# The last hidden tile's squares, mixes and split one down unit later, and two parts of the fourth tile loaded ahead of others

## The chip, the core and the metric

The kernel runs on one core of one Trainium2 chip. Its time is the time of the device for one execution, in microseconds, and the figure compared is the median of several executions. TensorE (PE in the profile, its weight loads PEld) multiplies, VectorE (DVE) and ScalarE (ACT) do elementwise work, GpSimd (POOL) and SyncE (SP) issue the transfers (DMAs) here. Each engine runs its own list of instructions strictly in order, and waits where a semaphore is not yet as far as an instruction asks.

## What is computed

One decoder layer for a prompt of 512 tokens and 32 sample tokens, 544 together: four token mixers (pooling, a gated recurrence, two kinds of attention), then an MLP. Only the MLP matters here:

```python
h = rms_norm(x, norm2_g)                              # 544 x 2048
hid = relu(einsum('btd,df->btf', h, w_up))            # 544 x 8192
x = x + einsum('btf,fd->btd', hid * hid, w_down)      # 544 x 2048
```

Everything is float32. Each operand of a product is split into a high and a low part in a type that TensorE takes (fp32r), and a product is three matmul passes: high by high, high by low, low by high.

## The kernel before

**Seven products.** Both matrix products of the MLP go by a scheme that makes four output blocks from seven products instead of eight, named P1 to P7. A unit is one pair of output row blocks: units 0 to 31 (UP_UNITS = 32) make the 8192 hidden rows, two blocks of 128 rows by two halves of 272 tokens each; units 32 to 79 are the down projection. A down unit is 48 accumulation windows of eight pairs of output rows: unit 32 + s works for the row pair s mod 8 on the hidden tiles of `window(s)`. A hidden tile is what one up unit leaves: its seven operands, high and low (128 x 7 x 2 x 272 numbers, 1904 KB). Windows grow slowly at first: unit 32 takes tiles 0 and 1, unit 33 tiles 0 to 2, units 34 and 35 tiles 0 to 3, unit 36 tiles 0 to 4, unit 37 tiles 2 to 6. The number of tiles in a window is the unit's depth, and a product of depth d is three groups of d matmuls of 128 x 272. An up unit has depth 8.

**The order of products** is the list RUN. Within a unit v it is P1, P2, P6, P5, P7, P4, and P3 of unit v comes behind P1 of unit v + 1, except at unit 31, whose P3 comes ahead of P1 of unit 32. So around the turn TensorE runs: P4(31), P3(31), P1(32), P2(32), P6(32), P5(32), P7(32), P4(32), P1(33), P3(32), P2(33), P6(33), P5(33), P7(33), P4(33), P1(34), P3(33), P2(34). ACT and DVE walk through the same list in loops of their own (from L1583 and L2221), and what they do at a position is done when that product is finished.

**What hangs on a product.** Its weight operand's high part is made by ACT (`op_high_part`) and its low part by DVE (`op_low_part`), both four products ahead, in a ring of four, so that they wait for the product four places before. At P1, P6 and P7 ACT copies the accumulated bank into `lines` (`copy_line`, waited for by P6, P7 and the ends). DVE makes the sums of weight blocks for the next unit (`sum_1` at P6, `sum_2` at P5, `sum_3` at P7, `sum_4` at P1) and the outputs (`first_ends` at P7, `second_ends` at P3). P3 of a unit waits for its `first_ends`.

**The hidden tile of an up unit v.** ACT takes its relu at P4(v) (`first_relu`) and its squares at P3(v): `first_squares` waits until the store of tile v - 1 has landed (`hid_stored`), since `hid_out` is one buffer, and then `second_squares`; four ACT instructions. DVE makes four differences at P2(v + 1) (`mix_hidden`), ACT the high part at P6(v + 1) (`hidden_high`), DVE the low part at P5(v + 1) (`hidden_low`), and POOL stores the tile to DRAM (`store_hidden`).

**POOL's queue at the turn** (L1172 to L1193). Each product's region of `hid_in` lies where the up products' operands lay, so a region is loaded when the last up unit's product of that name is done (`load_first(o)`, tiles 0 and 1 for product o). `load_part(i, r)` loads tile i for region r: region 0 is P1 and P2 together and region 1 is P6 and P5 (544 KB each), regions 2, 3, 4 are P7, P4, P3 (272 KB each). Unit 32's product o waits for its own `load_first`. P1 of a later unit waits for all five parts of each tile that its window adds (`hid_loaded`, L2633). POOL issues in order, and a wait holds what stands behind it.

Of the kernel before, what the change touches and what calls it, by code (L numbers as in the profile page):

```python
# [55 lines left out]
UP_UNITS, DOWN_UNITS, ROW_PAIRS = 32, 48, 8  # L56
# [14 lines left out]
def window(s):  # L71
    return OPENS[s], OPENS[s + ROW_PAIRS]
# [3 lines left out]
FIRST_TILES = window(0)[1]  # L76


def user_of(i):
    return max(s for s in range(DOWN_UNITS) if window(s)[0] <= i)  # L80
# [3 lines left out]
P1, P2, P6, P5, P7, P4, P3 = range(7)  # L84
# [62 lines left out]
def build_step(nc, xT, w_forget, weights, w_early, params, consts, dconsts, pool_w, lru_w, state_pool,  # L147
# [877 lines left out]
    def _(pool):  # L1025
# [20 lines left out]
        for g in range(GT):  # L1046
            w = 2 ** (g + 1)
            u = proj[:, U_POOL, g]
# [84 lines left out]
        def store_hidden(u):  # L1133
            pool.wait_ge(*hid_ready.at(u + 1))
            pool.dma_start(hid_parts[u], hid_out[:].bitcast(F32)).then_inc(hid_stored, 16)
# [3 lines left out]
        def load_first(o):  # L1139
            r, a = IN_AT[o]  # L1140
            pool.wait_ge(*product_done.at(AT[LAST, o] + 1))
            pool.dma_start(hid_in[r][:, a, 0:FIRST_TILES].bitcast(F32),
                           hid_parts[0:FIRST_TILES, :, o].rearrange("q p i n -> p q i n")).then_inc(first_in[o], 16)
# [3 lines left out]
        def load_part(i, r):  # L1147
            last = REGIONS[r][-1]
            if i < HID_SLOTS:
                pool.wait_ge(*product_done.at(AT[LAST, last] + 1))  # L1150
            else:
                pool.wait_ge(*product_done.at(AT[UP_UNITS + user_of(i - HID_SLOTS), last] + 1))
            q = i % UP_UNITS
            pool.wait_ge(hid_stored, 16 * (q + 1))
            o, n = REGIONS[r][0], len(REGIONS[r])
            pool.dma_start(hid_in[r][:, :, i % HID_SLOTS].bitcast(F32), hid_parts[q, :, o:o + n]  # L1156
                           ).then_inc(hid_loaded[i % HID_SLOTS].s, 16)

        def load_hidden(i, first=0):
            for r in range(first, len(REGIONS)):  # L1160
                load_part(i, r)
# [12 lines left out]
        load_first(P1)  # L1174
        load_first(P2)
        load_part(FIRST_TILES, 0)
        load_first(P6)
        load_first(P5)
        load_part(FIRST_TILES, 1)
        store_hidden(LAST - 1)  # L1180
        for o in (P7, P4, P3):
            load_first(o)
        load_hidden(FIRST_TILES, 2)
        load_hidden(FIRST_TILES + 1)
        store_hidden(LAST)
        added_rows = 0
        for i in range(FIRST_TILES + 2, HID_LOADS):
# [9 lines left out]
    def _(act):  # L1197
        own = Own(act, act_own)

        def f(out, in_, func, **kw):  # L1200
            return nc.scalar.activation(out, in_, func, **kw)  # L1201
# [277 lines left out]
        for i in range(UNITS - 1):  # L1479
            u, odd = divmod(i, 2)  # L1480
# [82 lines left out]
        def first_squares(v):  # L1563

            act.wait_ge(*a_relu.at(v + 1))
            if v:
                act.wait_ge(hid_stored, 16 * v)
            f(hid_f[:, 0:7:6], ends_a[:], ACT.Square).then_inc(a_squared.s, 1)

        def second_squares(v):  # L1570
            if v:
                act.wait_ge(*combined.at(2 * v + 2))
            f(ends_b[:], bank[:, 2:4, 0:HALF] if v == 0 else ends_b[:], ACT.Relu).then_inc(b_relu.s, 1)
            act.wait_ge(*b_relu.at(v + 1))
            f(hid_f[:, P2], ends_b[:, 1], ACT.Square).then_inc(b_squared.s, 1)
            f(ends_b[:, 0], ends_b[:, 0], ACT.Square).then_inc(b_squared.s, 1)

        def hidden_high(v):
            act.wait_ge(*hid_mixed.at(v + 1))
            f(hid_h, hid_f, ACT.Copy).then_inc(hid_high.s, 1)  # L1580

        for n, (v, o) in enumerate(RUN):
            if o == P1:  # L1583
                copy_line(v, n, ROOT_LINE)
            if o == P6:
                copy_line(v, n, MID_LINE)
            if o == P7:
                copy_line(v, n, TOP_LINE)
            if n + RING < len(RUN):
                op_high_part(n + RING)  # L1590
            if n in X_HIGH_AT:
                x_high(X_HIGH_AT[n])
            if n == len(PLAIN):
                act.wait_ge(*x_mixed.at(4))
                first_relu(0)
                first_squares(0)
                second_squares(0)
            if o == P4 and v < UP_UNITS:
                first_relu(v)
            if o == P3 and v < UP_UNITS:  # L1600
                first_squares(v)
                second_squares(v)
            if o == P6 and 1 <= v <= UP_UNITS:
                hidden_high(v - 1)


    @block.vector
    def _(dve):
        own = Own(dve, dve_own)
        v = nc.vector  # L1610
# [395 lines left out]
        for i in range(UNITS):  # L2006
            u, odd = divmod(i, 2)
# [179 lines left out]
        def mix_hidden(u):  # L2187
            dve.wait_ge(*a_squared.at(u + 1))
            dve.wait_ge(*b_squared.at(2 * u + 2))
            v.tensor_tensor(hid_f[:, P5], ends_b[:, 0], hid_f[:, P1], ALU.subtract).then_inc(hid_first.s, 1)  # L2190
            v.tensor_tensor(hid_f[:, P7], hid_f[:, P3], ends_b[:, 0], ALU.subtract).then_inc(hid_first.s, 1)
            dve.wait_ge(*hid_first.at(2 * u + 1))
            v.tensor_tensor(hid_f[:, P6], hid_f[:, P3], hid_f[:, P5], ALU.subtract).then_inc(hid_second.s, 1)
            dve.wait_ge(*hid_second.at(u + 1))
            v.tensor_tensor(hid_f[:, P4], hid_f[:, P2], hid_f[:, P6], ALU.subtract).then_inc(hid_mixed.s, 1)

        def hidden_low(u):
            dve.wait_ge(*hid_high.at(u + 1))
            v.tensor_tensor(hid_f, hid_f, hid_h.bitcast(F32), ALU.subtract).then_inc(hid_ready.s, 1)
# [21 lines left out]
        for n, (u, o) in enumerate(RUN):  # L2221
            if o == P7:
                first_ends(u)
            if o == P3:
                second_ends(u)
            if n in X_LOW_AT:
                x_low(X_LOW_AT[n], x_dif[X_LOW_AT[n]][:])
            if n + RING < len(RUN):
                op_low_part(n + RING)
            if n == X_MIX_AT:  # L2230
                dve.wait_ge(*product_done.at(len(PLAIN)))
                dve.wait_ge(*x_mixed.at(2))
                mixed(P6, x_dif[P7][:], quarter(0, 0), ALU.add)
                dve.wait_ge(*x_mixed.at(3))
                dve.wait_ge(*x_op_low.at(X_LOW_ORDER[X01]))
                mixed(P4, quarter(1, 0), x_dif[P6][:])
            if o == P1:
                sum_4(u)
            if o == P2 and 1 <= u <= UP_UNITS:
                mix_hidden(u - 1)  # L2240
            if o == P2 and u > UP_UNITS + ROW_PAIRS:
                join_b(u - 1)
            if o == P5 and 1 <= u <= UP_UNITS:
                hidden_low(u - 1)
            if o == P4 and u >= UP_UNITS + ROW_PAIRS:
                join_a(u)
            if u + 1 < UNITS_MLP and o in (P6, P5, P7):
                {P6: sum_1, P5: sum_2, P7: sum_3}[o](u + 1)
# [579 lines left out]
```

## Time and profile before

| | us |
|---|---|
| median of 3 runs | 2364.02 |
| lowest and highest | 2363.35, 2364.27 |
| the profiled execution's own time | 2367.05 |
| its span in the trace | 2365.4 |

The span begins with the first instruction of the profile, and all times of day below are microseconds from it. The last up unit ends at about 1678, and the down units run from there to the end. A timeline row gives start, duration, engine, source line, what is written from what, how many instructions are merged, and in brackets the engine's idle time before it with what ended that. Matmul ends are modelled and overlap the next start, so the pace of TensorE is read from one start to the next. PEclk is the clock that TensorE was granted, as a share of its full 2.4 GHz; 0.50 is 1.2 GHz.

### The profile page before, as it was taken

To read this page: it belongs to the slowest core of one execution; us is meant where nothing else is said; L and a number is where in the kernel's file an instruction comes from. 1 tells how busy PE (TensorE), PEld (TensorE's weight loads), DVE (VectorE), ACT (ScalarE), POOL (GpSimd) and SP (SyncE) were. 2 spreads that over 40 slices of the span, in tenths; PEclk is the share of its full clock that TensorE was granted. 3 is DMA by queue.
4 is the path that set the end of the run, shared out by engine and by line. 5 is a ranking of instruction groups with operands and counts; after the bars stand their busy time and mean duration, and the time that the engine had idled before them with its cause. 6 is when DMAs were issued, how large, how long until landed. Compare 5 with 4: busy or idle time off the path is not lost.

```text
span 2365.4 us, 44263 instructions
## 1 busy us (share of the span) xinstructions
PE 2310.8 (98%) x17398; PEld 2139.8 (90%) x17398; DVE 1625.6 (69%) x2166; ACT 1109.5 (47%) x1698; POOL 389.9 (16%) x658
## 2 busy tenths in 40 slices
PE   8999999999999999799999999999999999999999
PEld 7999999955555669789999999999899999999999
DVE  6355445444354465688888888888777888887887
ACT  6244445533333352356555555556544444444443
POOL 0061000154555510000000000000311111110200
PEclk9999999999999999899999999999999999999999
DMA  6332232599999976135555555554995657564643
GB/s 194 108 95 91 79 108 90 197 349 378 362 382 356 371 295 232 65 107 205 198 191 196 181 198 201 194 193 169 365 285 186 225 169 231 173 214 156 242 143 116
DMA packets 147809, 490.25 MB, mean 207 GB/s; under 512 B 28906, under 2 KB 32619, under 8 KB 136467
## 3 DMA queue, kind: packets, MB, share of 16 engines
q1 hardware_dynamic: 92418, 250.70, 31.3%
q0 software_dynamic: 55184, 236.73, 27.5%
q8 instruction: 139, 2.28, 0.4%
q14 instruction: 68, 0.55, 0.1%
HBM read 408.43 MB, written 78.91 MB: 206 GB/s over the span
## 4 chain that ended last, share of the span: by engine, by line
PE 93%; DVE 4%; DMA 1%; ACT 1%; issue 1%; SPq 0%; ACTq 0%; DVEq 0%
PE bank L2639 18%; PE bank L2642 18%; PE bank L2635 18%; PE bank L583 12%; PE bank L588 6%; PE bank L605 4%; PE bank L2524 4%; PE bank L2499 3%; PE bank L2459 2%; PE bank L2401 1%; DMA w_raw<-weights 1%; PE bank L2301 1%; PE bank L2430 1%; PE bank L2507 1%; PE bank L2415 1%
## 5 line engine op out<-in xcount | busy, mean ns | idle before, releaser
L583 PE MATMUL bank<-x_act,w_hi 128*128 128x364 f32 (+1 forms) x1728 | 377.4, 329 | 1.2 <-DVE w_lo L574 1.1
L2635 PE MATMUL bank<-hid_in,down_ring 128*128 128x272 f32 x1792 | 280.3, 288 | 5.9 <-issue 3.3
L2642 PE MATMUL bank<-hid_in,down_ring 128*128 128x272 f32 x1792 | 279.9, 288 | 0.0
L2639 PE MATMUL bank<-hid_in,down_ring 128*128 128x272 f32 x1792 | 279.6, 288 | 0.0
L583 PEld LDWEIGHTS bank<-x_act,w_hi 128*128 128x128 f32 x1728 | 275.3, 188 | 2.7 <-DVE w_lo L574 1.4
L2639 PE MATMUL bank<-x_op,ring 128*128 128x272 f32 x1736 | 254.1, 288 | 4.5 <-DVE x_op L2139 4.5
L2635 PE MATMUL bank<-x_op,ring 128*128 128x272 f32 x1736 | 253.8, 288 | 1.1 <-ACT lines L1201 1.1
L2642 PE MATMUL bank<-x_op,ring 128*128 128x272 f32 x1736 | 253.7, 288 | 0.0
L2635 PEld LDWEIGHTS bank<-hid_in,down_ring 128*128 128x128 f32 x1792 | 246.7, 189 | 6.5 <-issue 3.5
L1201 ACT ACTIVATE lines<-bank 128x272 f32<-128x272 f32 x237 | 94.4, 398 | 336.5 <-PE bank L2642 336.4
L2642 PEld LDWEIGHTS bank<-hid_in,down_ring 128*128 128x128 f32 x1792 | 246.4, 189 | 0.0
L2639 PEld LDWEIGHTS bank<-hid_in,down_ring 128*128 128x128 f32 x1792 | 246.4, 189 | 0.0
L2639 PEld LDWEIGHTS bank<-x_op,ring 128*128 128x128 f32 x1736 | 232.0, 189 | 4.9 <-DVE x_op L2139 4.9
L588 PE MATMUL bank<-x_act,w_lo 128*128 128x272 f32 x1152 | 234.5, 290 | 0.0
L2635 PEld LDWEIGHTS bank<-x_op,ring 128*128 128x128 f32 x1736 | 231.9, 189 | 1.3 <-issue 1.3
L2642 PEld LDWEIGHTS bank<-x_op,ring 128*128 128x128 f32 x1736 | 231.8, 188 | 0.0
L2075 DVE TENSOR_TENSOR down_ring<-down_raw,down_ring 128x768 fp32r<-128x768 f32 (+4 forms) x192 | 166.1, 866 | 78.5 <-ACT down_ring L1201 78.5
L588 PEld LDWEIGHTS bank<-x_act,w_lo 128*128 128x128 f32 x1152 | 200.4, 189 | 2.8 <-issue 1.3
L2075 DVE TENSOR_TENSOR ring<-up_raw,ring 128x1024 fp32r<-128x1024 f32 x128 | 156.0, 1221 | 65.8 <-ACT ring L1201 65.8
L1201 ACT ACTIVATE down_ring<-down_raw 128x768 fp32r<-128x768 f32 (+4 forms) x192 | 147.9, 771 | 103.1 <-PE bank L2642 103.1
L1156 POOL DMA_DIRECT2D hid_in<-hid_parts x160 | 99.1, 626 | 438.4 <-PE bank L2642 434.1
L2075 DVE TENSOR_TENSOR down_ring<-down_sum,down_ring 128x768 fp32r<-128x768 f32 (+4 forms) x144 | 124.9, 868 | 51.1 <-ACT down_ring L1201 47.5
(315 smaller groups left out, 3635.6 us busy)
## 6 DMA issues: line engine op xcount, KB each, us to landing
up_raw<-w_up SPq DMA_DIRECT2D x128, 512.0 KB, 4.2
hid_parts<-hid_out POOLq DMA_DIRECT2D x32, 1904.0 KB, 6.5
w_raw<-weights SPq DMA_DIRECT2D x43, 1024.0 KB, 4.9
hid_in<-hid_parts POOLq DMA_DIRECT2D x71, 544.0 KB, 5.4
down_raw<-w_down SPq DMA_DIRECT2D x96, 384.0 KB, 4.2
v_ring<-sb_v POOLq DMA_DIRECT2D x128, 256.0 KB, 5.2
v_ring<-fox_v POOLq DMA_DIRECT2D x120, 256.0 KB, 4.8
hid_in<-hid_parts POOLq DMA_DIRECT2D x96, 272.0 KB, 4.0
```

The costliest lines, as they stand in the source:

```text
L583: ins = nc.tensor.matmul(bank[:, base + b, 0:n], hi, row[:, t:t + n], start=begin, stop=end)
L588: ins = nc.tensor.matmul(bank[:, base + b, 0:HALF], lo, row[:, t:t + HALF], start=False, stop=False)
L605: ins = nc.tensor.matmul(bank[:, base + h, 0:HALF], w, row[:, t:t + HALF], start=first, stop=(end and w is lo))
L1156: pool.dma_start(hid_in[r][:, :, i % HID_SLOTS].bitcast(F32), hid_parts[q, :, o:o + n]).then_inc(hid_loaded[i % HID_SLOTS].s, 16)
L1201: return nc.scalar.activation(out, in_, func, **kw)
L2075: v.tensor_tensor(part_of(n, 1), factor(u, o), part_of(n, 0).bitcast(F32), ALU.subtract).then_inc(op_low.s, 1)
L2459: ins = mm(bank[ROWS * j:ROWS * j + ROWS, 4], q_pad[x][:, b, a], k_ring[:, j, :, a], start=(x == 1 and a == 0), stop=(a == 3))
L2499: ins = mm(bank[ROWS * j:ROWS * j + ROWS, 6], pt_t[:, c, ROWS * j:ROWS * j + ROWS], v_ring[:, (4 * u + c) % V_SLOTS, j], start=(c == 0), s ...
L2524: ins = mm(bank[:, early_bank(i), 0:HALF], wo[t % 2][:, k], y, start=(k == 0), stop=(k == 2 * GT - 1))
L2635: mm(out, part_of(n, 0)[:, cols], operand(k)[:, 0], start=(first and k == 0), stop=False, skip_group_check=True)
L2639: mm(out, part_of(n, 0)[:, P * k:P * k + P], operand(k)[:, 1], start=False, stop=False, skip_group_check=True)
L2642: ins = mm(out, part_of(n, 1)[:, P * k:P * k + P], operand(k)[:, 0], start=False, stop=(k == last), skip_group_check=True)
```

## The change

In ACT's and DVE's loops the conditions are written anew so that for v = 31 alone (UP_UNITS - 1) the steps come at other positions: `first_squares` and `second_squares` at P4(32) instead of P3(31), `mix_hidden` at P2(33) instead of P2(32), `hidden_high` at P6(33) instead of P6(32), `hidden_low` at P5(33) instead of P5(32). `first_relu(31)` stays at P4(31). In POOL's queue the fourth tile's parts 0 and 1 are issued right behind the third tile's parts 0 and 1. Nothing is added or dropped, on any engine.

```diff
         load_part(FIRST_TILES, 0)
+        load_part(FIRST_TILES + 1, 0)
         load_first(P6)
         load_first(P5)
         load_part(FIRST_TILES, 1)
+        load_part(FIRST_TILES + 1, 1)
         store_hidden(LAST - 1)
         for o in (P7, P4, P3):
             load_first(o)
         load_hidden(FIRST_TILES, 2)
-        load_hidden(FIRST_TILES + 1)
+        load_hidden(FIRST_TILES + 1, 2)
         store_hidden(LAST)
...
-            if o == P3 and v < UP_UNITS:
-                first_squares(v)
-                second_squares(v)
-            if o == P6 and 1 <= v <= UP_UNITS:
-                hidden_high(v - 1)
+            if o == P3 and v < UP_UNITS - 1 or (v, o) == (UP_UNITS, P4):
+                last = min(v, UP_UNITS - 1)
+                first_squares(last)
+                second_squares(last)
+            if o == P6 and 1 <= v < UP_UNITS or (v, o) == (UP_UNITS + 1, P6):
+                hidden_high(min(v, UP_UNITS) - 1)
...
-            if o == P2 and 1 <= u <= UP_UNITS:
-                mix_hidden(u - 1)
+            if o == P2 and 1 <= u < UP_UNITS or (u, o) == (UP_UNITS + 1, P2):
+                mix_hidden(min(u, UP_UNITS) - 1)
...
-            if o == P5 and 1 <= u <= UP_UNITS:
-                hidden_low(u - 1)
+            if o == P5 and 1 <= u < UP_UNITS or (u, o) == (UP_UNITS + 1, P5):
+                hidden_low(min(u, UP_UNITS) - 1)
```

ACT's list at the turn, before. The first row is the high part for P5(32), made at P3(31); `ends_a` and `ends_b` are what the squares of tile 31 read, `lines` are the copies at P1(32) and P6(32), `down_ring` rows are high parts of weights (256 columns are of unit 32, 384 of unit 33), the last row is `hidden_high(31)`:

```order
L1201 ACTIVATE down_ring3_192<-down_sum0_187 128x256
L1201 ACTIVATE hid_out_171<-ends_a_173 128x2x272
L1201 ACTIVATE ends_b_172<-ends_b_172 128x544
L1201 ACTIVATE hid_out_171<-ends_b_172 128x272
L1201 ACTIVATE ends_b_172<-ends_b_172 128x272
L1201 ACTIVATE lines_170<-bank 128x272
L1201 ACTIVATE down_ring0_189<-down_raw2_181 128x256
L1201 ACTIVATE down_ring1_190<-down_raw3_182 128x256
L1201 ACTIVATE lines_170<-bank 128x272
L1201 ACTIVATE down_ring2_191<-down_raw4_183 128x384
L1201 ACTIVATE hid_out_171<-hid_out_171 128x7x272
```

ACT's list with the change, from the copy at P7(32) to `hidden_high(31)`; 512 columns are of unit 34:

```order
L1203 ACTIVATE lines_170<-bank 128x272
L1203 ACTIVATE down_ring0_189<-down_raw5_184 128x384
L1203 ACTIVATE down_ring1_190<-down_sum1_188 128x384
L1203 ACTIVATE hid_out_171<-ends_a_173 128x2x272
L1203 ACTIVATE ends_b_172<-ends_b_172 128x544
L1203 ACTIVATE hid_out_171<-ends_b_172 128x272
L1203 ACTIVATE ends_b_172<-ends_b_172 128x272
L1203 ACTIVATE lines_170<-bank 128x272
...
L1203 ACTIVATE lines_170<-bank 128x272
L1203 ACTIVATE down_ring1_190<-down_raw0_179 128x512
L1203 ACTIVATE hid_out_171<-hid_out_171 128x7x272
L1203 ACTIVATE down_ring2_191<-down_sum1_188 128x384
```

The four squares now stand between the high part for P6(33) and the copy at P1(33), and `hidden_high` between the high parts for P1(34) and P3(33).

DVE's list before, at P5(32) and P7(32): the low part for P3(32), `hidden_low(31)`, `sum_2(33)` and `first_ends(32)`:

```order
L2075 TENSOR_TENSOR down_ring3_192<-down_sum1_188,down_ring3_192 128x256
L2199 TENSOR_TENSOR hid_out_171<-hid_out_171 128x7x272
L2093 TENSOR_TENSOR down_sum1_188<-down_sum0_187,down_raw4_183 128x384
L2170 TENSOR_TENSOR rows0_193<-lines_170,bank 128x2x272
L2075 TENSOR_TENSOR down_ring0_189<-down_raw5_184,down_ring0_189 128x384
```

DVE's list with the change, from P2(33) to P7(33): the low part for P4(33), the four mixes, the low part for P1(34), `sum_1(34)`, the low part for P3(33), `hidden_low(31)`, `sum_2(34)`, `first_ends(33)`:

```order
L2078 TENSOR_TENSOR down_ring0_189<-down_raw7_186,down_ring0_189 128x384
L2193 TENSOR_TENSOR hid_out_171<-ends_b_172,hid_out_171 128x272
L2194 TENSOR_TENSOR hid_out_171<-hid_out_171,ends_b_172 128x272
L2196 TENSOR_TENSOR hid_out_171<-hid_out_171 128x272
L2198 TENSOR_TENSOR hid_out_171<-hid_out_171 128x272
L2078 TENSOR_TENSOR down_ring1_190<-down_raw0_179,down_ring1_190 128x512
L2089 TENSOR_TENSOR down_sum0_187<-down_raw2_181,down_raw3_182 128x512
L2078 TENSOR_TENSOR down_ring2_191<-down_sum1_188,down_ring2_191 128x384
L2202 TENSOR_TENSOR hid_out_171<-hid_out_171 128x7x272
L2096 TENSOR_TENSOR down_sum1_188<-down_sum0_187,down_raw0_179 128x512
L2173 TENSOR_TENSOR rows1_194<-lines_170,bank 128x2x272
```

So the whole chain from the mixes to `hidden_low` has moved from in front of `first_ends(32)` to in front of `first_ends(33)`.

## Rows read from the trace of the kernel before

**Rows 1.** The page, busy time and share of each engine

```profile
PE 2310.8 (98%) x17398; PEld 2139.8 (90%) x17398; DVE 1625.6 (69%) x2166; ACT 1109.5 (47%) x1698; POOL 389.9 (16%) x658
```

**Rows 2.** Timeline of PE at the turn: start, us, engine, operation, count, idle before

```profile
1679.47 0.41 PE L2642 MATMUL bank<-hid_in,down_ring 128*128 128x272 f32 x2
1683.18 0.79 PE L2635 MATMUL bank<-hid_in,down_ring 128*128 128x272 f32 x2 [3.30 <-issue]
...
1688.85 0.39 PE L2635 MATMUL bank<-hid_in,down_ring 128*128 128x272 f32 x1 [0.67 <-DMA hid_in<-hid_parts]
...
1691.89 0.49 PE L2635 MATMUL bank<-hid_in,down_ring 128*128 128x272 f32 x2 [1.89 <-ACT down_ring L1201]
...
1694.19 0.89 PE L2635 MATMUL bank<-hid_in,down_ring 128*128 128x272 f32 x3
1694.87 0.89 PE L2639 MATMUL bank<-hid_in,down_ring 128*128 128x272 f32 x3
...
1699.48 0.54 PE L2642 MATMUL bank<-hid_in,down_ring 128*128 128x272 f32 x3
1699.86 0.67 PE L2635 MATMUL bank<-hid_in,down_ring 128*128 128x272 f32 x4
...
1701.37 0.54 PE L2635 MATMUL bank<-hid_in,down_ring 128*128 128x272 f32 x3
```

**Rows 3.** Stretches: length, busy of PE, PEld, DVE, ACT, POOL; PEclk, DMA share, GB/s

```profile
1664.00:1666.00 2.00, 2.00 (x18) 2.00 (x17) 1.54 (x3) 0.43 (x1) 1.07 (x2) 1.00 0.65 121
...
1671.00:1672.00 1.00, 1.00 (x10) 1.00 (x10) 1.00 (x1) 0.00 (x0) 0.07 (x1) 1.00 0.90 148
...
1680.00:1700.00 20.00, 14.26 (x86) 13.88 (x87) 13.56 (x26) 11.19 (x23) 13.09 (x22) 0.83 1.03 411
```

**Rows 4.** Stretches with the lower clock, the same columns

```profile
1683.20:1686.50 3.30, 3.30 (x15) 3.30 (x16) 3.05 (x9) 1.72 (x5) 0.87 (x2) 0.50 1.03 409
...
1692.00:1696.20 4.20, 4.20 (x24) 4.20 (x25) 3.70 (x8) 1.74 (x4) 4.20 (x8) 0.67 1.07 435
```

**Rows 5.** Timeline of ACT at the turn

```profile
1680.81 0.66 ACT L1201 ACTIVATE hid_out<-ends_a 128x544 f32<-128x544 f32 x1 [1.97 <-DMA hid_parts<-hid_out]
...
1682.70 0.38 ACT L1201 ACTIVATE lines<-bank 128x272 f32<-128x272 f32 x1
...
1686.08 1.80 ACT L1201 ACTIVATE hid_out<-hid_out 128x1904 fp32r<-128x1904 f32 x1 [0.36 <-DVE hid_out L2195]
1687.78 0.40 ACT L1201 ACTIVATE down_ring<-down_sum 128x256 fp32r<-128x256 f32 x1
```

**Rows 6.** Timeline of DVE at the turn

```profile
1684.43 0.43 DVE L2190 TENSOR_TENSOR hid_out<-ends_b,hid_out 128x272 f32<-128x272 f32 x1
...
1688.55 2.14 DVE L2199 TENSOR_TENSOR hid_out<-hid_out 128x1904 f32<-128x1904 f32 x1
...
1691.07 0.71 DVE L2170 TENSOR_TENSOR rows<-lines,bank 128x544 f32<-128x544 f32 x1
```

**Rows 7.** POOL's load of tiles 0 and 1 for P7: issue, then landing

```profile
L1142 POOL DMA_DIRECT2D hid_in<-hid_parts x1: 707/707/707, 1673.2 to 1673.2; - x1
...
DMA to landing us min/median/max: 9.6/9.6/9.6
```

**Rows 8.** The third tile's last part, for P3: issue, then landing

```profile
L1156 POOL DMA_DIRECT2D hid_in<-hid_parts x1: 537/537/537, 1680.5 to 1680.5; - x1
...
DMA to landing us min/median/max: 8.3/8.3/8.3
```

**Rows 9.** The seventh tile's last part: issue, then landing

```profile
L1156 POOL DMA_DIRECT2D hid_in<-hid_parts x1: 539/539/539, 1700.1 to 1700.1; - x1
...
DMA to landing us min/median/max: 23.2/23.2/23.2
```

**Rows 10.** Timeline: POOL's last store, and PE's first group of unit 37

```profile
1690.98 0.55 POOL L1135 DMA_DIRECT2D hid_parts<-hid_out x1 [6.91 <-DVE hid_out L2199]
...
1733.29 0.79 PE L2635 MATMUL bank<-hid_in,down_ring 128*128 128x272 f32 x5
```

## The prediction

> **What bounds the kernel now.** I read the page's busy line first: PE is busy 98% of the span [rows 1], so outside a few places nothing but matmuls counts, and a change that adds or drops no instruction can act only where PE waits. Next PE's timeline at the turn from up to down, which shows three such places in 20 us [rows 2]: 3.30 us ahead of P6(32), 0.67 us inside P1(33), 1.89 us ahead of P3(32). Then, for each, the list of the engine that ended it.
>
> The 3.30 us: P6 waits for the line copy at P1(32). ACT made that copy at 1682.70, because the four squares of tile 31 stood ahead of it, and the first of these had waited until 1680.81 for the store of tile 30 [rows 5]. P1(32) was finished before P2(32)'s last group, which began at 1679.47 [rows 2], so the copy was over 3 us late.
>
> The 0.67 us: P1(33) reads the third tile, whose last part was issued at 1680.5 and landed 8.3 us later, at 1688.8 [rows 8]. PE went on at 1688.85 [rows 2].
>
> The 1.89 us: P3(32) waits for `first_ends(32)`, 0.71 us from 1691.07, and that stood on DVE behind `hidden_low(31)`, 2.14 us from 1688.55 [rows 6], which in turn stood behind ACT's `hidden_high(31)`, 1686.08 to 1687.8, and the high part made after it [rows 5].
>
> Beside these the clock: behind the first pause TensorE was granted 0.50 for 3.30 us, and in the 4.2 us from 1692.0 it was granted 0.67 [rows 4]. Half speed for 3.3 us loses 1.65 us; the second stretch loses 4.2 x (1 - 0.67) = 1.4 us. I take 1.4 us as the price of one such fall. Which rows can see the transfers: from 1680 to 1700 the DMA share is 1.03 at 411 GB/s [rows 3], so there the DMA engines are full and POOL's queue is drained in order of issue.
>
> **The squares.** With them gone from P3(31) the copy at P1(32) comes in time, and P6(32) and P5(32) run without a pause, up to about 1681.2. The four instructions and their wait for the store of tile 30 now stand at P4(32). What is next late there is not ACT but the loads. P7(32) needs its tiles 0 and 1, which landed at 1673.2 + 9.6 = 1682.8 before [rows 7], and P1(33) needs the third tile, 1688.8 [rows 8]. Before, the pause by the squares covered both; now they are what PE waits for. So the 3.30 us are not won: PE comes to P1(33) sooner and waits there. The squares (2.2 us on ACT) lie in that wait and cost nothing; if the loads came 4 us sooner they would hold P6(33)'s line copy.
>
> **The two parts.** They put 2 x 544 KB = 1.11 MB ahead of the third tile's last part in a queue that is full. Its pace there: from P7's load (1682.8) to that part (1688.8) lie P4's and P3's loads (544 KB each) and three parts of 272 KB, 1.95 MB in 6.0 us, 0.325 MB/us. With no gap to use the two parts cost 1.11 / 0.325 = 3.4 us. There are gaps: 121 GB/s from 1664 to 1666 and 148 in the one us from 1671, where 411 is possible [rows 3]: 0.58 and 0.26 MB. The first is over before most of the new part, issued at about 1665.1, can flow, so I count half of it: 0.29 + 0.26 = 0.55 MB fit, and 0.56 MB remain, 1.7 us. I take 1.8 us: the third tile lands at 1690.6. The bounds are no delay (1688.8, if all fits) and 3.4 us (1692.2). On the other side the fourth tile is complete no later than before, and was never waited for: the parts moved ahead buy nothing that PE waited for.
>
> The Trainium skill (DMA: Bandwidth & Descriptors, section "Anatomy of one DMA — SWDGE (gpsimd) path") gives the variable part of such a transfer as bytes over 436 GB/s. By it 1.11 MB alone would be 2.6 us, between my two bounds; the trace's queue is slower since SyncE's weight loads share the engines. It speaks against issuing bytes early that nobody waits for in a full queue.
>
> **The chain behind the squares moves one unit.** From P2(33) done, call it D, with lengths of [rows 5, 6]: ACT's high part and DVE's low part for P4(33) take 1.1 us. From the first mix to the start of P3 it took 1691.89 - 1684.43 = 7.46 us before, through mixes, `hidden_high`, high and low part of P3's weights, `hidden_low`, `sum_2`, `first_ends`. The same chain now has weight blocks of 384 and 512 columns where 256 and 384 were: I add 0.35 us in three steps. So P3(33) can start at D + 1.1 + 7.46 + 0.35 = D + 8.9. PE's own work between D and P3(33) is P6, P5, P7, P4 at 3 x 0.375 us (a group of three is 0.38 us [rows 2]) and P1(34), 1701.37 - 1699.86 = 1.51 us: 6.0 us. The pause ahead of P3 does not go, it moves from P3(32) to P3(33) and is 2.9 us instead of 1.89: unit 33's products are longer, but before the low clock and the late third tile had stretched them.
>
> **The sum.** The third tile lands at 1690.6. Behind it: the last 7 of P1(33)'s 9 matmuls at 0.125 us (the first two read tiles 0 and 1 and run before), P3(32)'s 6 and P2(33)'s 9: 2.7 us. PE did only P7(32) and P4(32) between 1681 and 1690, so this is at the low clock at first, as behind the first pause [rows 4]: 1.4 us more. D = 1690.6 + 2.7 + 1.4 = 1694.7. P3(33) starts at 1694.7 + 8.9 = 1703.6 instead of 1701.37 [rows 2]: 2.2 us later. Behind its pause of 2.9 us I count one fall of the clock, 1.4 us, where before unit 34 ran at full speed. After that I count nothing: in unit 34 DVE has only its own work again, behind which PE did not wait before [rows 2]. Sum: +2.2 + 1.4 = **+3.6 us**. On the profiled execution's own 2367.05 that gives 2370.7; the median of the runs is 3.0 us below that execution, and to the median the sum is 2364.02 + 3.6 = **2367.6 us**.
>
> **What else moves.** The last store is issued behind `hidden_low(31)`, at about D + 7.6 = 1702.3 instead of 1690.98 [rows 10], and everything behind it on POOL comes up to 11.3 us later, less the 4.6 us of backlog that it had before. The seventh tile's last part landed at 1700.1 + 23.2 = 1723.3 [rows 9]; 6.7 to 11.3 us later is 1730.0 to 1734.6. Unit 37, which needs it, started at 1733.29 [rows 10] and now starts near 1736.9, so this is hidden. It costs if the shift passes 13.6 us.
>
> **The rivals.**
> (a) The full queue price: the two parts use no gap. The tile lands at 1692.2, D is 1.6 us later: +5.2 us, and +6.6 with a second fall of the clock; 2369.2 to 2370.6. This is the case on the slower side. It decides from a landing at about 1691.8. For it: the DMA share of 1.03 over 20 us; against: the two gaps, 121 and 148 GB/s [rows 3].
> (b) The loads do not slip: tile three lands at 1688.8 and both falls of the clock cost what I say: D is 1.8 us earlier, +1.8 us; with no fall behind P3(33) +0.4, and with none at all -1.0: 2363.0 to 2365.8.
> (c) The deferral works: the chain does not hold P3(33), say since DVE gets through it in PE's wait for the tile. Then P3(33) starts at D + 6.0: with the tile at 1688.8 to 1690.6, 1698.9 to 1700.7, and no second fall: -2.5 to -0.7 us, 2361.5 to 2363.3. Against: DVE's mixes stand behind a low part that needs P2(33) finished, so they can't use the wait.
> (d) The late loads hold unit 37, by the point above: another 1 to 4 us on my sum, 2368.6 to 2371.6.
> (e) The change does not do what it says: PE waits ahead of P6(32) for something else as long as before. Then unit 32 is as before, the chain still moves to unit 33: within 1 us of my sum.
>
> **How the numbers follow.** My sum with its small variants (and e) 0.50, (a) 0.22, (b) 0.18, (c) 0.06, (d) 0.04. A measurement here can tell 0.2%, 4.7 us, from no change. Slower by more: (a) nearly whole, (d) whole, and a fifth of my own case, whose terms can be 1 us off: 0.34. Faster by more needs P3(33) before 1696.7, which is below even (c); I leave 0.04 for what I don't see. Within: 0.62. The range reaches from the bottom of (b), 2363.0, to the top of (a), 2370.9 with the rounding of its terms, and leaves out (c) and part of (d).
>
> **What would show it.** Right: no pause ahead of P6(32); P7(32) starting near 1684.5 behind a DMA; P1(33)'s third matmul at 1690 to 1691; P3(33) with a pause of 2 to 3 us behind `first_ends(33)`, which follows `hidden_low(31)` directly; the granted clock at 0.50 around 1690 to 1693 and again behind 1703; the last store at about 1702. Wrong: a third tile that lands at 1688 or sooner (the two parts are free), P3(33) without a pause (the chain is shorter than I count), or a pause of PE in units 36 and 37 (the late store costs).

## The result, and the profile with the change

| | before | with the change |
|---|---|---|
| median of 7 runs, us | 2364.83 | 2372.76 |
| lowest to highest, us | 2363.35 to 2367.99 | 2370.58 to 2373.22 |
| span of the profiled execution, us | 2365.4 | 2371.2 |
| from the start of P1(32) to the end of the span, us | 687.2 | 695.5 |

The ratio of the runs is 1.0029, with a 95% interval from 1.0019 to 1.0039: 4.5 to 9.2 us slower, some 6.9 us. The forecast was +3.6 us in a range of 2363.0 to 2370.9; the time lies above it.

P1(32) starts at 1678.22 in the trace of before and at 1675.74 in the one with the change. Up to there TensorE's work is the same in both, and in all the kernels of this study that start lies between 1675.7 and 1679.7, without any order by what was changed. So below, times are counted from the start of P1(32) of the same trace, and the last row of the table, the down part, is what one profiled execution says of a kernel: +8.3 us here.

The timeline of PE with the change, the places that answer to the pauses in [rows 2] (start, us, operation, idle before):

```profile
1675.74 0.41 PE L2638 MATMUL bank<-hid_in,down_ring 128*128 128x272 f32 x2
...
1684.29 0.79 PE L2638 MATMUL bank<-hid_in,down_ring 128*128 128x272 f32 x2 [5.37 <-DMA hid_in<-hid_parts]
...
1686.31 0.79 PE L2638 MATMUL bank<-hid_in,down_ring 128*128 128x272 f32 x2 [0.32 <-DMA hid_in<-hid_parts]
...
1691.38 0.59 PE L2638 MATMUL bank<-hid_in,down_ring 128*128 128x272 f32 x1 [2.93 <-DMA hid_in<-hid_parts]
...
1696.54 0.62 PE L2638 MATMUL bank<-hid_in,down_ring 128*128 128x272 f32 x3
...
1705.68 0.61 PE L2638 MATMUL bank<-hid_in,down_ring 128*128 128x272 f32 x3 [2.91 <-ACT down_ring L1203]
```

The pause ahead of P6(32) is gone. In its place PE waits 5.37 us ahead of P7(32), 0.32 ahead of P4(32) and 2.93 inside P1(33), each ended by a load, and 2.91 us ahead of P3(33) at 1705.68. The four pauses are 11.5 us, the three of before were 5.9.

The loads, issue then landing: POOL's load of tiles 0 and 1 for P7, and the third tile's last part (these answer to [rows 7] and [rows 8]):

```profile
L1142 POOL DMA_DIRECT2D hid_in<-hid_parts x1: 704/704/704, 1670.7 to 1670.7; - x1
...
DMA to landing us min/median/max: 13.5/13.5/13.5
```

```profile
L1156 POOL DMA_DIRECT2D hid_in<-hid_parts x1: 539/539/539, 1678.0 to 1678.0; - x1
...
DMA to landing us min/median/max: 13.3/13.3/13.3
```

P7's load landed 13.5 us after its issue instead of 9.6, so 3.9 us of delay were there already; the third tile's last part took 13.3 instead of 8.3. Counted from P1(32), PE could go on with the third tile at 15.6 us (1691.38) instead of 10.6 us (1688.85 against 1678.22).

The clock, in three stretches (length, busy of PE, PEld, DVE, ACT, POOL; PEclk, DMA share, GB/s), beside [rows 4]:

```profile
1684.30:1688.10 3.80, 3.48 (x14) 3.19 (x14) 2.32 (x5) 0.87 (x3) 0.00 (x0) 0.50 1.03 406
1691.30:1696.50 5.20, 5.12 (x22) 5.12 (x23) 2.12 (x4) 1.33 (x3) 0.00 (x0) 0.50 0.10 37
1706.80:1710.40 3.60, 3.60 (x18) 3.60 (x18) 2.98 (x5) 1.26 (x2) 3.60 (x7) 0.53 1.14 368
```

TensorE ran at 1.2 GHz in the first two and in nearly all of the third (0.53). The second lasted 5.2 us at a DMA share of 0.10: the queue that had held PE up until 1691 had run empty, since the next thing in it was the store behind `hidden_low(31)`.

The chain, as ACT and DVE ran it (it answers to [rows 5] and [rows 6]):

```profile
1699.46 1.80 ACT L1203 ACTIVATE hid_out<-hid_out 128x1904 fp32r<-128x1904 f32 x1 [0.59 <-DVE hid_out L2198]
1701.16 0.50 ACT L1203 ACTIVATE down_ring<-down_sum 128x384 fp32r<-128x384 f32 x1
```

```profile
1697.81 0.43 DVE L2193 TENSOR_TENSOR hid_out<-ends_b,hid_out 128x272 f32<-128x272 f32 x1
...
1702.17 2.13 DVE L2202 TENSOR_TENSOR hid_out<-hid_out 128x1904 f32<-128x1904 f32 x1
1704.22 0.69 DVE L2096 TENSOR_TENSOR down_sum<-down_sum,down_raw 128x512 f32<-128x512 f32 x1
1704.82 0.71 DVE L2173 TENSOR_TENSOR rows<-lines,bank 128x544 f32<-128x544 f32 x1
```

`hidden_low(31)` at 1702.17 now stands ahead of `first_ends(33)` at 1704.82, and P3(33) starts behind that.

### The profile page after: what moved, and what is told of

It is laid out like the page before. It is cut to its first block, busy times and chain, and to the rows that moved or that the text cites. A ratio compares the mean times of both kernels' runs of the same rounds, so it can differ in the third digit from the quotient of the medians.

```text
span 2371.2 us, 44263 instructions
## 1 busy us (share of the span) xinstructions
PE 2314.3 (98%) x17398; PEld 2142.9 (90%) x17398; DVE 1625.6 (69%) x2166; ACT 1109.7 (47%) x1698; POOL 391.0 (16%) x658
## 4 chain that ended last, share of the span: by engine, by line
PE 93%; DVE 4%; issue 1%; DMA 1%; ACT 1%; POOL 0%; SPq 0%; ACTq 0%; DVEq 0%; POOLq 0%
PE bank L2642 18%; PE bank L2645 18%; PE bank L2638 18%; PE bank L583 12%; PE bank L588 6%; PE bank L605 4%; PE bank L2527 4%; PE bank L2502 3%; PE bank L2462 2%; PE bank L2404 1%; PE bank L2304 1%; PE bank L2433 1%; PE bank L2510 1%; PE bank L2418 1%; DMA hid_in<-hid_parts 1%
## 5 line engine op out<-in xcount | busy, mean ns | idle before, releaser
L2638 PE MATMUL bank<-hid_in,down_ring 128*128 128x272 f32 x1792 | 281.4, 289 | 11.5 <-DMA hid_in<-hid_parts 8.6
L2638 PEld LDWEIGHTS bank<-hid_in,down_ring 128*128 128x128 f32 x1792 | 247.5, 190 | 12.5 <-ACT down_ring L1203 8.7
```

The source lines that it names most:

```text
L2638: mm(out, part_of(n, 0)[:, cols], operand(k)[:, 0], start=(first and k == 0), stop=False, skip_group_check=True)
```

## The experiments

Two things were moved at once, and the loads were later than either seemed to account for. The theory (L, with W for the weights) was that POOL's queue was full: what is put ahead of the third tile delays it by its bytes, and the pause that the deferral takes away also lets SyncE's weight loads go earlier into the same DMA engines. The rivals were that the deferral does it in another way, and that the moved parts fit into gaps. A second theory (C) was that the chain, from the mixes to `hidden_low(31)`, holds P3(33). In the table, "third tile" is when PE went on with it, counted from the start of P1(32), "P3(33)" when that product started, "down part" as above; these three are of one profiled execution each. The ratio, with its interval, is that of 8 to 11 executions (7 for the change) against the kernel before; four kernels ran once, and have none.

| kernel | third tile | P3(33) | down part | ratio |
|---|---|---|---|---|
| before | 10.6 | 23.2 | 687.2 | |
| the change | 15.6 | 29.9 | 695.5 | 1.0029 (1.0019 to 1.0039) |
| e1_defer | 11.6 | 25.2 | 690.8 | 1.0025 (1.0014 to 1.0036) |
| e2_parts | not waited for | 26.4 | 690.8 | 1.0017 (1.0007 to 1.0026) |
| e4_spread | 11.9 | 22.2 | 687.2 | 1.0006 (0.9996 to 1.0015) |
| e5_late_store | 8.1 | 16.9 | 685.5 | 0.9999 (0.9990 to 1.0009) |
| e6_roomier | 8.1 | 18.5 | 687.7 | 1.0004 (0.9995 to 1.0013) |
| e7_part0 | 13.4 | 27.0 | 692.5 | one execution |
| e3_hold | 12.5 | 25.0 | 690.5 | one execution |
| e10_defer_hold | 9.3 | 22.9 | 688.5 | one execution |
| e11_parts_spread | 14.2 | 25.0 | 690.3 | one execution |
| e8_earlier | 8.2 | 19.6 | 684.9 | 0.9988 (0.9979 to 0.9998) |
| e9_both | 7.5 | 25.5 | 693.2 | 1.0021 (1.0012 to 1.0030) |

### e1_defer: the deferral without the moved parts

Against the change:

```diff
         load_part(FIRST_TILES, 0)
-        load_part(FIRST_TILES + 1, 0)
...
         load_part(FIRST_TILES, 1)
-        load_part(FIRST_TILES + 1, 1)
...
-        load_hidden(FIRST_TILES + 1, 2)
+        load_hidden(FIRST_TILES + 1)
```

> The change with POOL's queue put back: the fourth tile's two parts come behind the third tile again, the squares, mixes and split stay one unit later. Theory L (in the full queue the two parts delay the third tile by about 4 us, and the weight loads that the removed pause lets go earlier by about 1 us): the third tile lands some 14.0 us after P1(32) starts (10.6 before, 15.6 in the change, counted from that start), so about 1 us later than before and 4 us sooner than in the change; the pause ahead of P3(33) stays near 2.9 us; the time is 2 to 4.5 us above before and 3.5 to 5 us below the change. Rival theory D (the deferral itself makes the loads late): the third tile lands as late as in the change and the time is that of the change, about 7 us above before.

The third tile came at 11.6 us, 1.0 later than before and 4.0 sooner than in the change, as L has it; the 14.0 us in the expectation does not agree with its own two differences. PE's pauses in e1:

```profile
1681.99 0.49 PE L2636 MATMUL bank<-hid_in,down_ring 128*128 128x272 f32 x2 [1.34 <-ACT down_ring L1201]
1683.91 0.49 PE L2636 MATMUL bank<-hid_in,down_ring 128*128 128x272 f32 x2 [0.93 <-DMA hid_in<-hid_parts]
1689.07 0.59 PE L2636 MATMUL bank<-hid_in,down_ring 128*128 128x272 f32 x1 [3.92 <-DMA hid_in<-hid_parts]
1702.66 0.79 PE L2636 MATMUL bank<-hid_in,down_ring 128*128 128x272 f32 x3 [2.95 <-ACT down_ring L1201]
```

The deferral by itself loses: the 3.30 us that it takes away ahead of P6(32) come back as 6.2 us ahead of the third tile (1.34, 0.93, 3.92, where there was 0.67), and the pause ahead of P3 is 2.95 us, instead of 1.89. The 1.34 us ahead of P7(32) is put down to ACT, but P7's load was issued at 1672.4 and landed 9.4 us later, at 1681.8, just ahead of PE's start at 1681.99, so both came together. The down part is 3.6 us longer than before, the change's is 8.3. The ratio says more, 5.9 us, above the 2 to 4.5 expected and only 1 us below the change's 6.9, where 3.5 to 5 were expected.

### e2_parts: the moved parts without the deferral

The kernel before, with the change's lines in POOL's queue alone:

```diff
         load_part(FIRST_TILES, 0)
+        load_part(FIRST_TILES + 1, 0)
...
         load_part(FIRST_TILES, 1)
+        load_part(FIRST_TILES + 1, 1)
...
-        load_hidden(FIRST_TILES + 1)
+        load_hidden(FIRST_TILES + 1, 2)
```

> The kernel before with only POOL's queue changed: the two parts of the fourth tile ahead, squares, mixes and split as before. Theory L: the store of tile 30 lands 4 us later, so the first square waits until about 6.5 us after P1(32) starts instead of 2.6, the pause ahead of P6(32) grows from 3.3 to about 7.3 us, the pause ahead of P3(32) stays near 1.9: 4 to 5 us above before. Rival theory D: the parts fit into gaps of the queue, the pause ahead of P6(32) grows by less than 1 us, the time is within 1 us of before.

The pause ahead of P6(32), and the first square of tile 31 on ACT:

```profile
1685.35 0.79 PE L2637 MATMUL bank<-hid_in,down_ring 128*128 128x272 f32 x2 [6.56 <-issue]
```

```profile
1682.99 0.66 ACT L1203 ACTIVATE hid_out<-ends_a 128x544 f32<-128x544 f32 x1 [5.23 <-DMA hid_parts<-hid_out]
```

The pause ahead of P6(32) grew from 3.30 to 6.56 us, and D (no more than 1 us) is out. It is a little less than the 7.3 expected: the first square, which waits for the store of tile 30, began 5.9 us after P1(32) instead of 2.6, so the parts cost that store 3.3 us, not 4. The down part is 3.6 us longer, the ratio says 4.0. By the down parts the two halves add to 7.2 of the change's 8.3 us; by the ratios they add to 9.9 where the change has 6.9, each uncertain by 2 to 3 us. So both halves lose, and how the loss divides is known to no better than that.

### e7_part0: one of the two parts

```diff
-        load_part(FIRST_TILES + 1, 1)
...
-        load_hidden(FIRST_TILES + 1, 2)
+        load_hidden(FIRST_TILES + 1, 1)
```

> The change, with only the fourth tile's part 0 ahead of the others; part 1 comes behind the third tile, as before. Theory F (no gap: each part of 544 KB put into the queue costs its share): the third tile lands 13.4 to 14.0 us after P1(32) starts, halfway between e1_defer (11.6) and the change (15.6). Rival theory G (the gap at the time part 0 is issued swallows it, as the prediction had half of it): 11.6 to 12.6 us, as in e1_defer, and nearly all of the delay comes with part 1.

13.4 us, between 11.6 and 15.6: the first part, issued where the prediction saw the larger gap, cost 1.8 us in this one trace, close to what F expects. Two traces of nearly one order differ by up to 1.4 us (below), so G, up to 12.6 us, is made unlikely by it and not ruled out.

### e3_hold and e10_defer_hold: the weight loads held

In SyncE's loop, once on the change (e3_hold) and once on e1_defer (e10_defer_hold):

```diff
                 i, _ = piece_slot(v, b)
+                if (v, b) == (UP_UNITS + 2, A11):
+                    sp.wait_ge(*product_done.at(AT[UP_UNITS, P7] + 1))
                 if v >= UP_UNITS + 2:
```

> The change, with SyncE's weight loads for unit 34 held until P7(32) is finished. Theory W (the pause that the deferral removed let these loads, 3 x 256 KB and more, go some 3 us sooner, ahead of the third tile, which costs about 1 us): the third tile lands 0.7 to 2 us sooner after P1(32) starts than in the change (15.6 us), P7(32) starts at most 0.5 us sooner. Rival theory V (they make no difference, the further 1 us is the spread between executions): 15.2 to 16.0 us.

> e1_defer (squares and chain one unit later, POOL's queue as before) with SyncE's weight loads for unit 34 held until P7(32) is finished. Theory W (what the deferral alone does to the third tile is that these loads go earlier): it lands no later than before, 9.5 to 10.8 us after P1(32) starts, against 11.6 in e1_defer; the pause ahead of P3(33) stays near 3 us. If it lands at 11.6 again, the deferral's 1 us has another source or is spread between executions.

Why these loads at all: the three weight loads for unit 34 around the turn, in the trace of before (first) and with the change (second), issues and landing:

```profile
L1015 SPq DMA_DIRECT2D down_raw<-w_down x3: 328/438/482, 1683.9 to 1684.8; - x3
DMA to landing us min/median/max: 6.3/7.9/9.4
```

```profile
L1015 SPq DMA_DIRECT2D down_raw<-w_down x3: 328/523/611, 1677.9 to 1678.9; - x3
DMA to landing us min/median/max: 10.5/12.0/13.2
```

Before, they were issued 5.7 us after P1(32) started, since their slots were freed by low parts behind the pause; with the change 2.2 us after it. Held, the third tile came at 12.5 us on the change and at 9.3 us on e1: sooner than expected in both (13.6 to 14.9, and 9.5 to 10.8). The kernels e11 and e4 have the same transfers as the change and e1 up to the third tile's, though they put tiles 4 to 6 behind them at once; taken as second traces without the hold, they have 14.2 and 11.9 beside 15.6 and 11.6. By the means the hold gains 14.9 - 12.5 = 2.4 us with the parts ahead and 11.75 - 9.3 = 2.4 us without, and the two parts cost 14.9 - 11.75 = 3.2 us without the hold and 12.5 - 9.3 = 3.2 us with it. Since the two traces of a pair differ by up to 1.4 us, either figure may be off by about 1 us.

The hold takes more out of the way than the deferral put in: it also keeps back unit 34's first load, which before and change alike issue 1 to 2 us ahead of P1(32). So it shows that weight loads ahead of the tile cost it time, 2.4 us for four of them. For the deferral's own share e10 is the closest to before: its four loads went out 5.2 to 6.6 us after P1(32), where before has three of them, and there the tile was not late. What the deferral adds, three of them 3.5 us earlier, is the difference of e1 and e4 to before: 1.0 to 1.3 us, which is no more than two traces can differ by. W holds in its sign; the size of this share is not settled.

### e4_spread and e11_parts_spread: the chain taken apart

On e1_defer and on the change:

```diff
-            if o == P6 and 1 <= v < UP_UNITS or (v, o) == (UP_UNITS + 1, P6):
+            if o == P6 and 1 <= v < UP_UNITS or (v, o) == (UP_UNITS + 1, P4):
...
-            if o == P5 and 1 <= u < UP_UNITS or (u, o) == (UP_UNITS + 1, P5):
+            if o == P5 and 1 <= u < UP_UNITS or (u, o) == (UP_UNITS + 2, P2):
...
-        store_hidden(LAST)
...
         for i in range(FIRST_TILES + 2, HID_LOADS):
+            if i == HID_SLOTS:
+                store_hidden(LAST)
```

> As e1_defer, with the chain behind the squares taken apart: the mixes stay at P2(33), the high part of tile 31 is made at P4(33) and its low part at P2(34), and the store of tile 31 is issued behind the loads of tiles 4 to 6. Theory C (the chain mixes, high part, low part holds first_ends(33) and so P3(33)): no pause ahead of P3(33) and no second fall of the clock, 3.5 to 4.5 us below e1_defer, so within 1.5 us of before. Rival theory N (P3(33) is late for another reason, such as the third tile's weights landing late): the pause stays above 2 us and the time is that of e1_defer.

> The change with both moved parts ahead, but the chain behind the squares taken apart as in e4_spread (high part at P4(33), low part at P2(34), last store behind the loads of tiles 4 to 6). If the two costs add: the third tile lands 15 to 16 us after P1(32) starts as in the change, no pause ahead of P3(33), P1(32) to the end 690 to 692.5 us against 695.5 in the change. If the chain's pause only took the place of a wait for loads behind it, a pause of similar length shows elsewhere up to unit 37 and the down part is 694 to 696 us.

No pause ahead of P3(33) in either. Ahead of P3(34) there is now one of 0.6 us (e4's shown):

```profile
1712.22 0.74 PE L2637 MATMUL bank<-hid_in,down_ring 128*128 128x272 f32 x4 [0.61 <-ACT down_ring L1202]
```

The down part of e4 is 3.6 us shorter than e1's and equal to before's (687.2), e11's 5.2 us shorter than the change's (1.4 us of that is its earlier third tile). So C holds: the chain is worth 3.6 to 3.8 us (4.5 by the ratios of e1 and e4), the pause and part of a fall of the clock. For e11 a third tile at 15 to 16 us was expected and it came at 14.2; its down part is in the expected range. With the chain apart and the loads in their old order the deferral is free, and still gains nothing: 1.0006.

### e5_late_store, e6_roomier, e8_earlier: a deferral that frees the queue

If the queue is what binds, the deferral's one use is that the store of tile 30 (1904 KB) need no longer go ahead of the loads. On e1_defer:

```diff
-        store_hidden(LAST - 1)
         for o in (P7, P4, P3):
             load_first(o)
         load_hidden(FIRST_TILES, 2)
         load_hidden(FIRST_TILES + 1)
-        store_hidden(LAST)
+        store_hidden(LAST - 1)
```

with the last store behind the loads of tiles 4 to 6, as in e4, in e6 and e8 a wait of POOL for P2(34) ahead of tile 5, and tile 31's steps placed as follows:

| | squares | mixes | high part | low part |
|---|---|---|---|---|
| e5_late_store | P2(34) | P7(34) | P4(34) | P2(35) |
| e6_roomier | P4(34) | P3(34) | P2(35) | P4(35) |
| e8_earlier | P5(34) | P4(34) | P1(35) | P2(35) |

> The deferral carried on to where it frees the queue: the store of tile 30 (1904 KB) is issued behind the loads of tiles 2 and 3 instead of ahead of P7's loads, the squares of tile 31 come at P2(34), its mixes at P7(34), its high part at P4(34), its low part at P2(35), and its store behind the loads of tiles 4 to 6. Theory L: the third tile lands 4 to 5 us sooner than in e1_defer; P7(32) does not wait, P1(33) waits 1 to 3 us, no pause ahead of P3(32) or P3(33), at most one fall of the clock: 5 to 8 us below before. If the queue's order is not what holds the third tile, it lands as in e1_defer and the time is within 1.5 us of e4_spread.

The third tile came 3.5 us sooner than in e1 and P3(33) started 6.2 us sooner than before. But the 5 to 8 us expected did not come: 4.5 of the 6.2 us were given back in units 34 to 36, 3.6 of them in four pauses that had not been there (three shown; the fourth is 1.14 us ahead of P3(35), at 1718.42):

```profile
1699.31 0.73 PE L2637 MATMUL bank<-hid_in,down_ring 128*128 128x272 f32 x4 [0.61 <-ACT lines L1202]
...
1704.87 0.73 PE L2637 MATMUL bank<-hid_in,down_ring 128*128 128x272 f32 x4 [0.84 <-ACT down_ring L1202]
...
1709.11 0.74 PE L2637 MATMUL bank<-hid_in,down_ring 128*128 128x272 f32 x4 [1.01 <-ACT lines L1202]
```

> As e5_late_store, whose gain of 6.2 us up to P3(33) was given back in units 34 to 36. Now the squares come at P4(34), the mixes at P3(34), the high part at P2(35), the low part at P4(35), and the loads of tiles 5 and 6 wait for P2(34). Theory L with a reason for the give-back (each of tile 31's steps stood where a line copy or an output was needed soon, and the weight loads were slow in a queue filled with tiles 5 and 6): no pause over 0.4 us behind the third tile's, P1(32) to the end 5 to 6.5 us shorter than before (687.2 us), ratio 0.997 to 0.998. If the give-back has another source, the down part is within 2 us of that of e5_late_store (685.5 us).

A miss. One pause is left in unit 34 (0.47 us), but the high part at P2(35) waited 2.86 us for mixes that stood behind other work on DVE, and a line copy behind it held PE for 2.7 us:

```profile
1715.71 1.79 ACT L1204 ACTIVATE hid_out<-hid_out 128x1904 fp32r<-128x1904 f32 x1 [2.86 <-DVE hid_out L2199]
1717.41 0.38 ACT L1204 ACTIVATE lines<-bank 128x272 f32<-128x272 f32 x1
```

and the clock fell twice, behind the third tile and behind that pause.

> As e6_roomier, with tile 31's steps placed by what e6's trace showed (the high part at P2(35) waited for mixes behind two low parts and held a line copy, 2.7 us): squares at P5(34), mixes at P4(34), high part at P1(35), low part at P2(35), last store some 33 to 36 us after P1(32) starts. Theory L: the third tile lands 8.1 us after P1(32) starts as in e5 and e6, no pause over 0.5 us behind it, P1(32) to the end 681.5 to 684 us (before 687.2), by 1.5 us depending on whether the clock falls behind the 3 us pause in P1(33): ratio 0.997 to 0.9985. If tile 31's steps cost about the same wherever they stand, 685 to 688 us.

```profile
1681.85 0.49 PE L2639 MATMUL bank<-hid_in,down_ring 128*128 128x272 f32 x2 [0.18 <-DMA hid_in<-hid_parts]
...
1685.94 0.60 PE L2639 MATMUL bank<-hid_in,down_ring 128*128 128x272 f32 x1 [2.85 <-DMA hid_in<-hid_parts]
...
1719.60 0.74 PE L2639 MATMUL bank<-hid_in,down_ring 128*128 128x272 f32 x4 [1.03 <-DVE rows L2174]
```

One pause of 1.03 us is left behind the third tile's, where none over 0.5 was expected. The down part is 684.9 us, a little above the 681.5 to 684 expected, the ratio 0.9988 with an interval up to 0.9998: the only version whose interval lies below the kernel before, by some 3 us, with an upper end that all but touches no change.

### e9_both: e8_earlier with the weights held

```diff
+                if (v, b) == (UP_UNITS + 2, A11):
+                    sp.wait_ge(*product_done.at(AT[UP_UNITS, P4] + 1))
```

> e8_earlier with SyncE's weight loads for unit 34 held until P4(32) is finished. Theory W (weight loads in the full queue cost the third tile time): it lands 0.7 to 2.5 us sooner than in e8_earlier, at 5.6 to 7.4 us after P1(32) starts, and the down part is 0.5 to 2 us shorter, unless the held weights come late for sum_1(34), which would show as a pause ahead of P1(34) or P3(33). Rival theory V (no effect on the tile): 8.1 us and the time of e8_earlier.

```profile
1684.71 0.59 PE L2641 MATMUL bank<-hid_in,down_ring 128*128 128x272 f32 x1 [2.55 <-DMA hid_in<-hid_parts]
...
1702.67 1.02 PE L2641 MATMUL bank<-hid_in,down_ring 128*128 128x272 f32 x3 [7.67 <-ACT down_ring L1206]
```

The third tile came 0.7 us sooner, and the held weights then came too late, the pause that the expectation had named: 7.67 us ahead of P3(33), which turned a gain of 0.12% into a loss of 0.21%. Once PE is early, the wait can't be afforded.

## Why the prediction was wrong

**Right.** The squares' pause goes; the loads take its place; the four squares lie in PE's wait for the third tile and end no pause where they now stand. The chain: from the end of P2(33) to P3(33) I had 8.9 us and a pause of 2.9; P6(33) started at 1696.54 and P3(33) at 1705.68, 9.1 us, with a pause of 2.91. The fall of the clock behind it: the down part beyond P3(33) is 1.5 us longer than before (8.3 - 6.8), I had 1.4. The fourth tile's early parts bought nothing. Unit 37 was not held: its last load was issued at 1713.7 and landed 22.1 us later, at 1735.8, and P1(37) started at 1739.15 without a pause, though with 3.3 us left where I had 2.3 to 6.9.

**The step that failed: "I take 1.8 us: the third tile lands at 1690.6."** It came 5.0 us later than before, past my upper bound of 3.4. P7(32), for which my sign was 1684.5, 6.3 us after P1(32), came at 8.6: 2.3 of the missing 3.2 us were there before the third tile's last part was due. Two faults are in the step. First the gaps: I let 0.55 MB of the moved 1.11 MB fit into stretches of 121 and 148 GB/s. e7 has the first part costing 1.8 us, and the hold experiment puts the two parts at 3.2 us, close to the 3.4 that the queue's own pace gave before I took the gaps off. That was rival (a), and it should have been the main case.

The traces show what became of the gaps. Before (first two rows) and with the change (last two), the one us from 7 us ahead of P1(32), and the 8 us up to P1(32), the columns as in [rows 3]:

```profile
1671.22:1672.22 1.00, 1.00 (x11) 1.00 (x10) 1.00 (x1) 0.00 (x0) 0.00 (x0) 1.00 0.70 161
1670.22:1678.22 8.00, 8.00 (x66) 8.00 (x65) 4.25 (x7) 1.67 (x4) 2.82 (x5) 1.00 1.00 383
```

```profile
1668.74:1669.74 1.00, 1.00 (x11) 1.00 (x10) 1.00 (x1) 0.00 (x0) 0.55 (x1) 1.00 1.04 410
1667.74:1675.74 8.00, 8.00 (x66) 8.00 (x65) 4.24 (x7) 1.67 (x4) 3.52 (x6) 1.00 1.04 380
```

The first gap took up next to nothing: from 14.2 to 12.2 us ahead of P1(32) the rate was 125 GB/s before and 128 with the change. The second was filled, 161 became 410 GB/s. But over the 8 us the mean rate did not rise, 383 and 380 GB/s (399 in e11): what flowed in the gap was lost to slower stretches behind it. With one part ahead (e7) the mean did rise, to 427, and its third tile was later all the same. Why the rate fell behind the filled gap, and why e7's bytes did not help, no run here tells.

Second, a term that was not in the sum. The deferral takes away a pause, DVE's low parts come sooner, and with them the slots for unit 34's weights: SyncE's loads go 3.5 us earlier into engines that are already full, ahead of the third tile. I listed POOL's queue and missed that SyncE's issues hang on the same work. Against before, e1 and e4 give it 1.0 to 1.3 us. With the parts' 3.2 that is 4.2 to 4.5, where the two traces with the parts ahead (the change and e11) show 5.0 and 3.6 more than before. That weight loads ahead of the tile delay it is shown by e3 and e10; how the 5.0 us divide between the parts, these loads and the spread between executions is known to about 1 us only.

**The term that was mis-sized: the first fall of the clock.** I took 1.4 us, from [rows 4]. The granted clock was 0.50 for the whole 5.2 us from the third tile to P6(33), which took 1696.54 - 1691.38 = 5.16 us where I had 2.7 + 1.4 = 4.1: 1.1 us more. Before, the low clock in unit 33 came later and lasted shorter: 0.82 was granted from 1692.0 to 1694.2, 0.50 from there to 1696.2 and 0.89 from there to 1699.0. Here P1, P3 and P2 all fell into it.

Put together by the prediction's own steps, in the profiled execution: 3.2 us more for the tile (5.0 where I had 1.8), 1.1 for the clock, 0.2 for the chain, on +3.6 makes +8.1, where the down part says +8.3. That it closes so well is in part luck, since the ratio of the runs says 6.9, somewhere between 4.5 and 9.2.

**The chances.** The case of a full queue price had 0.22 and +5.2 to +6.6 us, "slower" 0.34. The measured interval, 4.5 to 9.2 us, has nearly all of itself on that side.

## What to carry to other kernels

When a pause is taken away, list every queue whose next issue hangs on work behind the pause, not only the one that the change edits: those transfers go earlier too, and where the DMA engines are full they push back what the engine will wait for next. In such a stretch price moved bytes at the queue's own pace, and make that the main case: here a gap that was filled, 161 GB/s becoming 410, still brought nothing forward that stood behind it. Deferring work helps only if something that bound the path is freed by it: here the squares had to be deferred far enough for the 1904 KB store to go behind the loads, and a chain through two engines has to be taken apart on its new place, not moved whole.

## What the runs showed of the hardware

The clock's fall behind a pause of 3 us is no fixed price. In e5_late_store and e6_roomier PE did the same work ahead of the same pause of 3.14 us in P1(33), which ended 8.1 us after P1(32) in both. These are the 3 us behind it in e5 (first) and e6 (second), PEclk being the third figure from the end:

```profile
1684.00:1687.00 3.00, 2.97 (x23) 2.97 (x24) 0.94 (x2) 1.28 (x3) 3.00 (x6) 1.00 1.02 394
```

```profile
1687.75:1690.75 3.00, 2.96 (x14) 2.96 (x15) 0.38 (x1) 0.81 (x2) 1.36 (x3) 0.56 1.04 404
```

In e5 the full clock was granted all along, up to P3(33) at 16.9 us; in e6 it fell, and P3(33) started at 18.5 us. So one profile of such a place can be off by 1.5 us against the next, which is the size of most of what was compared here.

Two traces with the same transfers up to the third tile's (the change and e11_parts_spread) had it at 15.6 and 14.2 us, while e1 and e4, a pair of the same kind, agreed within 0.3. In e11 and e4 the loads of tiles 4 to 6 were issued behind it while it was still on its way. Whether that or the spread between executions made the 1.4 us was not tried.
